# A hybrid attention layer on eight cores: the merge of the previous tile is written ahead of the GLA projections, and the order planner counts memory at 270 GB/s

## The chip, the cores and the metric

The kernel runs on the 8 cores of one Trainium2 chip. Each core works on one sequence of the batch of 8, and no core needs anything of another. The metric is the device time of the slowest core, in microseconds (us). Before the change it was 1416.05 us as the median of 3 runs (1414.8 to 1484.5).

## The reference

One decoder layer with two branches that share one input projection. For each token the columns of `w_in` give queries, keys, values and a gate for a causal differential attention with ALiBi (4 heads, two maps of 64), and queries, keys, values, a gate and a low-rank decay for gated linear attention (GLA, 4 heads, state 64 x 128). Both branch outputs are normed, gated, projected up, and merged under two sigmoid gates; an output projection, a norm and the residual follow.

```python
h = rms_norm(x, g_pre)
qa, ka, va, za, qb, kb, vb, zb, lr, gate_a, gate_b = split(h @ w_in)        # 1024 -> 5648
oa = diff_attention(qa, ka, va, lam, slopes)                                # causal, over all 4096 positions
ya = (rms_norm(oa, g_sub_a) * (1 - lam_init) * silu(za)) @ w_up_a           # 512 -> 1024
glog = log_sigmoid(lr @ w_alpha + b_alpha) / 16
ob = gla_chunked(qb, kb, vb, glog)                                          # a state carried from chunk to chunk
yb = (rms_norm(ob, g_sub_b) * silu(zb)) @ w_up_b                            # 512 -> 1024
y = sigmoid(gate_a) * ya + sigmoid(gate_b) * yb
out = x + rms_norm(y @ w_out, g_post)                                       # 1024 -> 1024
```

## The kernel before

**Tiles and stages.** The 4096 tokens of a core are worked in 8 tiles of 512, `t` = 0 to 7. A tile passes through these stages: `stage_a` (load x, norm, transpose to `hT`), `stage_batt` (the attention's Q, K and V projections, 96 matmuls of 512 columns), `stage_za` (the gate of the attention, 32), `stage_glaproj` (GLA's values, queries with keys, and gate: 32 each, and in a stream of its own the low-rank decay, 10), `stage_gla` (four chunks of 128 tokens that run through a state: in each, two matmuls for the scores, two for the new state, eight for the output), `stage_att` (attention of the tile over all keys so far: in batches of 8 score matmuls at L837, two exponentials on ACT at L845, then the matmuls into `acc`), `stage_e` (the merge: per column `j` of 8, two gate groups of 8 matmuls, then two up-projection groups of 4) and `stage_f` (output projection, 64 matmuls, norm, residual and store). `stage_e` and `stage_f` of tile t-1 run during tile t; those of tiles 0 and 1 both run during tile 2.

**Who sets the order.** The program does not issue instructions as it records them. `_Prog.op` records each with its duration on each engine that may take it, and `schedule` places them one by one: of all that are ready, the one that can start first; among those that start alike, the one with the lowest `prio`. A stream has a stretch of the plan, set by `P.at(begin, end, name)` in tiles, and `prio` runs linearly from begin to end by the PE work recorded in that stream so far. `fill(t)` is the stream from t to t+1 into which `stage_za`, `stage_glaproj`, `stage_e`, `stage_f` and the next tile's `stage_batt` are recorded one after the other, so the order of the calls in the main loop is the order of their due times; attention has the stretch t to t+1 as a stream of its own, the decay ("g") and GLA's chunks ("c") have theirs. What comes out is one fixed order for each engine and one for SP, which issues all DMAs.

**How a DMA is planned.** One transfer after the other, each `nbytes` at a fixed rate behind the one before, and 1.8 us until it has landed (L242). The rate decides only the order; it moves no data.

**Buffers that the steps touch.** Projections go through two PSUM banks (`pg`): a group fills one, ACT or DVE empties it. Scores use four banks (`qk`), written by a batch once both exponentials of the batch before have read them; `acc` has two. A weight chunk of 1 MB (bf16) lives in `wbuf`, three buffers from tile 2 on. The first time a chunk is needed it is converted (`convert`): eight f32 pieces of 256 KB through staging buffers in `KT`, each scaled by DVE, ACT or POOL, then stored to `wsc`, from where every later use loads it (`acquire`). GLA needs its keys transposed by DMA (`khat`, from `ktT`).

The softmax here doesn't subtract the row's maximum and nothing guards it: scores larger than these inputs give would overflow.

## Time and profile before

| | us |
|---|---|
| median of 3 runs | 1416.05 |
| fastest of them | 1414.8 |
| the profiled execution, whole | 1419.39 |
| span of its slowest core (core 1), first to last instruction | 1417.8 |
| spans of the other cores | 1399.1 to 1412.5 |
| PE busy on core 1 | 1329.9 |
| ACT busy | 830.6 |
| DVE busy | 742.2 |

The profile's page shows one execution on its slowest core. Engines are PE (matmul), PEld (weight load, beside PE), DVE, ACT, POOL and SP (DMA issue). Busy times are unions, and a matmul's end is modelled, so that the spacing of matmuls is read from start to start. Line L511 is a helper that records every matmul but the scores (L837); what a matmul is can be told from its tiles: `ps_pg<-sb_hT,sb_wbuf` is a projection by token rows (values, gates z, V), `ps_pg<-sb_wbuf,sb_hT` one by columns (Q, K, merge gates), `ps_pg<-sb_gaT,sb_wbuf` and `sb_gbT` the up-projections, `ps_pg<-sb_wbuf,sb_yT` the output projection, `ps_acc<-sb_V,sb_PT` attention's second matmul, `ps_pg<-sb_qtT,sb_ktT`, `sb_vb,sb_khat`, `sb_stbf,sb_qtT` and `sb_vb,sb_ATs` the four kinds of a GLA chunk. In the first tiles some buffers lie in the space of `KT`, `V` and `yT`, so `sb_V` can stand for `hT` or `gbT`, and `sb_yT` for a weight buffer.

### The profile page before, as it was taken

The numbers are of one execution on the slowest core, as the hardware profiler recorded it, in microseconds if no ns is written. First come the engines' busy times: TensorE is split into PE (matmuls) and PEld (weight loads), VectorE is DVE, ScalarE is ACT, GpSimd is POOL, SyncE is SP. The second block draws the span as 40 slices with busy tenths as digits, with TensorE's granted clock in tenths as the row PEclk, the third lists the DMA queues.
The fourth block names the chain that finished last, engine by engine and source line by source line (L and its number), as shares of the span: only waits on it lengthen the run. The fifth ranks groups of instructions, "written<-read, shape, count | busy, mean of one in ns | idle before, by whom it ended". The sixth has DMA issues, their size and how long they took to land.

```text
span 1417.8 us, 30361 instructions; the slowest of 8 cores (1399.1 to 1417.8 us)
## 1 busy us (share of the span) xinstructions
PE 1329.9 (94%) x10784; PEld 735.3 (52%) x10784; DVE 742.2 (52%) x2211; ACT 830.6 (59%) x1134; POOL 201.4 (14%) x309
## 2 busy tenths in 40 slices
PE   4997999999989999999989999999999999999996
PEld 2344454444545555545555555555555555666542
DVE  4488675666753557344472354643355624344634
ACT  4454556444535557475574766758666768767721
POOL 2142121010210012000120011210011200110100
PEclk9999999999999999999999999999999999999998
DMA  8995538955684328514294142743325722321443
GB/s 255 283 268 160 144 95 260 252 171 166 179 235 175 127 98 236 174 60 131 93 257 153 61 131 94 208 165 98 95 97 137 236 72 70 108 78 64 161 171 119
DMA packets 120099, 217.44 MB, mean 153 GB/s; under 512 B 73472, under 2 KB 82064, under 8 KB 105744
## 3 DMA queue, kind: packets, MB, share of 16 engines
q1 hardware_dynamic: 119952, 215.51, 50.3%
q8 instruction: 89, 1.46, 0.4%
q14 instruction: 58, 0.48, 0.1%
HBM read 166.72 MB, written 32.51 MB: 141 GB/s over the span
## 4 chain that ended last, share of the span: by engine, by line
PE 82%; DMA 6%; DVE 4%; issue 3%; ACT 3%; SPq 2%; POOL 0%; DVEq 0%; ACTq 0%; POOLq 0%
PE ps_pg L511 57%; PE ps_acc L511 15%; PE ps_qk L837 9%; DMA sb_KT<-w_in 2%; DMA sb_xr<-x 2%; ACT sb_PT L845 2%; DMA sb_khat<-sb_ktT 1%; SPq L488 1%; SPq L588 1%; DMA sb_wbuf<-wsc 1%; DVE sb_xr L974 0%; DMA sb_KT<-w_up_a 0%; DVE sb_szB L682 0%; DMA sb_KT<-w_out 0%; DMA wsc<-sb_wbuf 0%
## 5 line engine op out<-in xcount | busy, mean ns | idle before, releaser
L845 ACT ACTIVATE sb_PT<-ps_qk 128x1024 bf16<-128x1024 f32 (+1 forms) x544 | 518.0, 997 | 200.4 <-PE ps_qk L837 186.1
L511 PE MATMUL ps_acc<-sb_V,sb_PT 128*128 128x129 bf16 x4224 | 401.5, 221 | 8.2 <-ACT sb_PT L845 4.3
L511 PE MATMUL ps_pg<-sb_hT,sb_wbuf 128*128 128x512 bf16 x1536 | 392.3, 381 | 4.3 <-DVE sb_szB L682 1.3
L511 PEld LDWEIGHTS ps_acc<-sb_V,sb_PT 128*128 128x128 bf16 x4224 | 308.1, 98 | 139.5 <-issue 32.3
L511 PE MATMUL ps_pg<-sb_wbuf,sb_hT 128*128 128x512 bf16 x864 | 225.6, 380 | 4.5 <-DVE sb_szB L682 3.2
L511 PEld LDWEIGHTS ps_pg<-sb_hT,sb_wbuf 128*128 128x128 bf16 x1536 | 142.9, 98 | 150.9 <-issue 30.1
L837 PE MATMUL ps_qk<-sb_QT,sb_KT 64*128 64x256 bf16 (+1 forms) x2176 | 162.9, 269 | 10.9 <-ACT sb_PT L845 10.5
L945 DVE SCALAR_TENSOR_TENSOR sb_tmp<-sb_tmp,ps_pg 128x512 f32<-128x512 f32 x128 | 87.8, 686 | 142.5 <-PE ps_acc L511 85.7
L930 ACT ACTIVATE sb_tmp<-ps_pg 128x512 f32<-128x512 f32 x128 | 76.4, 597 | 131.3 <-PE ps_pg L511 98.2
L891 POOL TENSOR_TENSOR sb_statE<-sb_statE,sb_mhalf 128x1 f32<-128x1 f32 x128 | 75.0, 591 | 380.3 <-DVE sb_statE L889 369.7
L837 PEld LDWEIGHTS ps_qk<-sb_QT,sb_KT 64*128 64x128 bf16 x2176 | 84.5, 94 | 76.1 <-issue 57.5
L511 PEld LDWEIGHTS ps_pg<-sb_wbuf,sb_hT 128*128 128x128 bf16 x864 | 80.4, 98 | 80.8 <-issue 15.8
L511 PE MATMUL ps_pg<-sb_wbuf,sb_yT 128*128 128x512 bf16 x448 | 116.2, 385 | 5.3 <-DVE sb_tmp L965 2.2
L850 POOL TENSOR_SCALAR_AFFINE_SELECT sb_PT<-sb_PT 128x512 bf16<-128x512 bf16 x64 | 43.1, 673 | 501.9 <-ACT sb_PT L845 499.4
L511 PE MATMUL ps_pg<-sb_V,sb_wbuf 128*128 128x512 bf16 x288 | 70.9, 396 | 7.0 <-DVE sb_wbuf L595 1.5
L962 ACT ACTIVATE sb_tmp<-ps_pg 128x512 f32<-128x512 f32 x64 | 38.2, 597 | 50.4 <-PE ps_pg L511 33.9
L511 PEld LDWEIGHTS ps_pg<-sb_wbuf,sb_yT 128*128 128x128 bf16 x448 | 41.2, 99 | 48.3 <-issue 16.7
L511 PE MATMUL ps_pg<-sb_gbT,sb_wbuf 128*128 128x512 bf16 x224 | 61.8, 379 | 1.8 <-DVE sb_ste L792 0.7
L511 PE MATMUL ps_pg<-sb_gaT,sb_wbuf 128*128 128x512 bf16 x224 | 62.7, 380 | 0.1
L965 DVE TENSOR_TENSOR sb_tmp<-ps_pg,sb_gpost 128x512 f32<-128x512 f32 x64 | 43.9, 688 | 36.1 <-ACT sb_tmp L962 35.9
L681 ACT ACTIVATE sb_tmp<-ps_pg 128x512 f32<-128x512 f32 x64 | 37.9, 601 | 39.7 <-PE ps_acc L511 21.6
L893 DVE SCALAR_TENSOR_TENSOR sb_gatedA<-sb_oaf,sb_statE,sb_szA 128x128 bf16<-128x128 f32 x128 | 45.7, 360 | 21.6 <-POOL sb_statE L891 20.6
(135 smaller groups left out, 1260.6 us busy)
## 6 DMA issues: line engine op xcount, KB each, us to landing
sb_wbuf<-wsc SPq DMA_DIRECT2D x94, 1024.0 KB, 5.4
sb_KT<-w_in SPq DMA_DIRECT2D x88, 256.0 KB, 8.7
sb_xr<-x SPq DMA_DIRECT2D x36, 512.0 KB, 5.1
out<-sb_xr SPq DMA_DIRECT2D x32, 512.0 KB, 3.2
sb_xa<-x SPq DMA_DIRECT2D x28, 512.0 KB, 6.0
wsc<-sb_wbuf SPq DMA_DIRECT2D x14, 1024.0 KB, 7.0
sb_KT<-w_out SPq DMA_DIRECT2D x16, 256.0 KB, 4.5
sb_yT<-wsc SPq DMA_DIRECT2D x2, 1024.0 KB, 10.1
```

Of the source, the lines that this page charges most:

```text
L488: return P.op({"sp": (0.38, 0.0)}, lambda e: e.dma_start(out=fn_out(), in_=src), reads=reads, writes=writes, dma=sem, nbytes=nbytes)
L511: return P.op(_pe(n), lambda e: e.matmul(out=out_f(), lhsT=lf(), rhs=rf(), start=start, stop=stop, **kw), reads=reads, writes=writes, mode ...
L681: P.op({"act": _act(512, True)}, lambda e: e.activation(out=tmp[z.i][:], in_=pg[b.i][:], func=AF.Tanh, scale=0.5), table="tanh", reads=[b] ...
L837: lambda e, kb=kb, m=m, kbi=kbi, ca=ca, n=n: e.matmul(out=qk[:, 2 * half + m, kbi * 256:kbi * 256 + n], lhsT=KT[64 * m:64 * m + 64, h, kb ...
L845: P.op({"act": (0.075 + width / 600.0, 0.1)}, lambda e: e.activation(out=PT[pt.i][:, :, 0:width], in_=qk[:, 2 * half:2 * half + 2, 0:width ...
L850: return e.affine_select(out=v, in_=v, pattern=[[0, 2], [0, 2], [1, 128]], compare_op=ALU.is_ge, fill=0.0, base=0, channel_multiplier=-1)
L891: P.op({"pool": (0.45, 0.1)}, lambda e: e.tensor_tensor(out=statE[st.i][:, 4:5], in0=statE[st.i][:, 3:4], in1=mhalf[:, 0:1], op=ALU.pow), ...
L893: P.op({"dve": _dve(128, 1.0, 1)}, lambda e: e.scalar_tensor_tensor(out=gatedA[:, blk, h * 128:(h + 1) * 128], in0=oaf[o2.i][:], scalar=st ...
L930: P.op({"act": _act(512, True)}, lambda e, b=b, z=z: e.activation(out=tmp[z.i][:], in_=pg[b.i][:], func=AF.Tanh, scale=0.5), table="tanh", ...
L945: P.op({"dve": _dve(512)}, lambda e, b=b, z=tg[ab]: e.scalar_tensor_tensor(out=tmp[z.i][:], in0=tmp[z.i][:], scalar=1.0, in1=pg[b.i][:], o ...
L962: P.op({"act": (0.571, 0.02)}, lambda e, b=b, z=z, st=st, hh=hh: e.activation(out=tmp[z.i][:], in_=pg[b.i][:], func=AF.Square, accum_out=s ...
L965: P.op({"dve": _dve(512)}, lambda e, b=b, z=z, hh=hh: e.tensor_tensor(out=tmp[z.i][:], in0=pg[b.i][:], in1=gpost[:, hh * 512:(hh + 1) * 51 ...
```

## The change

In the main loop `stage_e` of the tiles `us` moves from behind GLA to the place between `stage_za(t)` and `stage_glaproj(t)`; `stage_f` stays behind GLA. The decay stream is due from t+0.3 to t+0.5 instead of t-0.05 to t+0.15, GLA's chunks from t+0.55 to t+1 instead of t+0.25 to t+0.95. The two chunks of `w_out` are no longer converted at the start of tile 2 but where `stage_f` first asks for them, so that tile 2 does not load them from `wsc` again. The planner's rate for transfers goes from 300 to 270 GB/s. Matmuls are the same 10784.

```diff
             if o.is_dma:
-                dma_free = max(dma_free, free[e]) + o.nbytes / 300e3
+                dma_free = max(dma_free, free[e]) + o.nbytes / 270e3
                 o.fin = dma_free + 1.8
...
-            P.at(t - 0.05, t + 0.15, "g")
+            P.at(t + 0.3, t + 0.5, "g")
...
         def stage_gla(t):
-            P.at(t + 0.25, t + 0.95, "c")
+            P.at(t + 0.55, t + 1, "c")
...
+            us = [u for u in (((), (), (0, 1))[t] if t < 3 else (t - 1,)) if u < ntiles]
             if t < ntiles:
                 stage_za(t)
-            if t == 2:
-                for c in (W_O, W_O + 1):
-                    convert(c, (0, 0.5))
+            if us:
+                stage_e(us, t)
             if t < ntiles:
                 stage_glaproj(t)
                 stage_gla(t)
                 fill(t)
-            us = [u for u in (((), (), (0, 1))[t] if t < 3 else (t - 1,)) if u < ntiles]
             if us:
-                stage_e(us, t)
                 stage_f(us)
```

What the two programs issue is shown at three places.

PE at the end of attention of tile 4 (scores in `ps_qk`, second matmuls in `ps_acc`, the Q projection of tile 5 as `ps_pg<-sb_hT,sb_wbuf`, or GLA's outputs from `sb_stbf` and `sb_ATs`); before:

```order
L837 MATMUL ps_qk<-sb_QT,sb_KT 128x256 x8
L511 MATMUL ps_acc<-sb_V,sb_PT 128x129 x6
L837 MATMUL ps_qk<-sb_QT,sb_KT 128x256 x8
L511 MATMUL ps_acc<-sb_V,sb_PT 128x129 x24
L511 MATMUL ps_pg<-sb_hT,sb_wbuf 128x512 x51
```

and with the change:

```order
L837 MATMUL ps_qk<-sb_QT,sb_KT 128x256 x8
L511 MATMUL ps_pg<-sb_hT,sb_wbuf 128x512 x8
L511 MATMUL ps_pg<-sb_stbf,sb_qtT 128x128
L511 MATMUL ps_acc<-sb_V,sb_PT 128x129 x5
L511 MATMUL ps_pg<-sb_vb,sb_ATs 128x128
L511 MATMUL ps_acc<-sb_V,sb_PT 128x129 x6
L511 MATMUL ps_pg<-sb_stbf,sb_qtT 128x128
L511 MATMUL ps_acc<-sb_V,sb_PT 128x129 x3
L837 MATMUL ps_qk<-sb_QT,sb_KT 128x256 x8
L511 MATMUL ps_pg<-sb_hT,sb_wbuf 128x512 x8
```

Before, two score batches have only six matmuls between them and the next tile's projections come behind the attention; with the change a projection group of eight stands between the same batches.

PE at the last two GLA chunks of tile 0 (the gate projection z of GLA is `ps_pg<-sb_wbuf,sb_V` here); before:

```order
L511 MATMUL ps_pg<-sb_vb,sb_khat 128x256 x2
L837 MATMUL ps_qk<-sb_QT,sb_KT 128x256 x6
L837 MATMUL ps_qk<-sb_QT,sb_KT 128x128 x2
L511 MATMUL ps_pg<-sb_stbf,sb_qtT 128x128
L511 MATMUL ps_pg<-sb_vb,sb_ATs 128x128
L511 MATMUL ps_pg<-sb_stbf,sb_qtT 128x128
L511 MATMUL ps_pg<-sb_vb,sb_ATs 128x128
L511 MATMUL ps_pg<-sb_stbf,sb_qtT 128x128
L511 MATMUL ps_pg<-sb_vb,sb_ATs 128x128
L511 MATMUL ps_pg<-sb_stbf,sb_qtT 128x128
L511 MATMUL ps_pg<-sb_vb,sb_ATs 128x128
L511 MATMUL ps_pg<-sb_wbuf,sb_V 128x512 x16
```

and with the change:

```order
L511 MATMUL ps_pg<-sb_wbuf,sb_V 128x512 x4
L511 MATMUL ps_pg<-sb_qtT,sb_ktT 128x256 x2
L511 MATMUL ps_pg<-sb_wbuf,sb_V 128x512 x4
L511 MATMUL ps_pg<-sb_vb,sb_khat 128x256 x2
L511 MATMUL ps_pg<-sb_wbuf,sb_V 128x512 x5
L511 MATMUL ps_pg<-sb_stbf,sb_qtT 128x128
L511 MATMUL ps_pg<-sb_vb,sb_ATs 128x128
L511 MATMUL ps_pg<-sb_stbf,sb_qtT 128x128
L511 MATMUL ps_pg<-sb_vb,sb_ATs 128x128
L511 MATMUL ps_pg<-sb_stbf,sb_qtT 128x128
L511 MATMUL ps_pg<-sb_wbuf,sb_V 128x512
L511 MATMUL ps_pg<-sb_vb,sb_ATs 128x128
```

The last sixteen matmuls of the gate projection, which stood behind the last chunk, stand between its steps.

SP at the start of tile 2, where weights are converted for the first time (`w_out` is the output projection, `w_in` in 2x256 the merge's gates, `w_up_a` and `w_up_b` the up-projections); before:

```order
L588 DMA sb_KT<-w_out 128x512 x8
L520 DMA_TRANSPOSE sb_gbT<-sb_gatedB 128x4x128
L588 DMA sb_KT<-w_out 128x512
L627 DMA wsc<-sb_wbuf 128x4096
L588 DMA sb_KT<-w_out 128x512 x2
L520 DMA_TRANSPOSE sb_gaT<-sb_gatedA 128x4x128
L588 DMA sb_KT<-w_out 128x512
L520 DMA_TRANSPOSE sb_gaT<-sb_gatedA 128x4x128
L588 DMA sb_KT<-w_out 128x512
L603 DMA sb_wbuf<-wsc 128x4096
L588 DMA sb_KT<-w_out 128x512 x3
L603 DMA sb_wbuf<-wsc 128x4096
```

and with the change:

```order
L588 DMA sb_KT<-w_in 128x2x256 x8
L520 DMA_TRANSPOSE sb_gbT<-sb_gatedB 128x4x128
L588 DMA sb_KT<-w_up_a 128x512 x4
L627 DMA wsc<-sb_wbuf 128x4096
L588 DMA sb_KT<-w_up_b 128x512
L520 DMA_TRANSPOSE sb_gbT<-sb_gatedB 128x4x128
L588 DMA sb_KT<-w_up_b 128x512 x3
L520 DMA_TRANSPOSE sb_gaT<-sb_gatedA 128x4x128 x2
L520 DMA_TRANSPOSE sb_gbT<-sb_gatedB 128x4x128
L627 DMA wsc<-sb_wbuf 128x4096
L588 DMA sb_KT<-w_in 128x2x256 x8
```

The merge's first two chunks take the place of the output projection's, and the two loads for GLA's projections that stood among them stand later.

## Rows read from the trace of the kernel before

**Rows 1.** The page, span and part 1: busy us, share, instructions
```profile
span 1417.8 us, 30361 instructions; the slowest of 8 cores (1399.1 to 1417.8 us)
PE 1329.9 (94%) x10784; PEld 735.3 (52%) x10784; DVE 742.2 (52%) x2211; ACT 830.6 (59%) x1134; POOL 201.4 (14%) x309
```
**Rows 2.** Windows: stretch, its us, busy us (count) by engine, PE clock, DMA, GB/s
```profile
0.00:40.00 40.00, 18.45 (x107) 9.67 (x108) 18.47 (x48) 19.51 (x31) 8.69 (x18) 0.99 0.92 260
40.00:120.00 80.00, 75.58 (x454) 36.09 (x453) 55.54 (x181) 38.66 (x57) 21.90 (x31) 0.96 1.06 270
120.00:200.00 80.00, 69.34 (x498) 36.71 (x500) 59.39 (x221) 39.29 (x56) 17.09 (x25) 0.93 0.39 114
200.00:400.00 200.00, 189.53 (x1290) 97.94 (x1290) 131.16 (x366) 99.81 (x150) 27.89 (x40) 0.99 0.69 200
400.00:760.00 360.00, 344.58 (x2715) 190.01 (x2714) 183.88 (x552) 208.64 (x293) 51.21 (x78) 1.00 0.52 159
760.00:1320.00 560.00, 549.57 (x5229) 326.19 (x5227) 248.60 (x747) 391.12 (x488) 67.44 (x104) 1.00 0.36 115
1320.00:1418.00 98.00, 82.85 (x503) 38.69 (x501) 45.13 (x100) 33.59 (x62) 7.17 (x13) 0.95 0.43 152
```
**Rows 3.** Waits of PE: who waited for whom, us, times, longest
```profile
PE ps_qk L837 <- ACT sb_PT L845: 10.5, 17, 1.5
PE ps_acc L511 <- ACT sb_PT L845: 4.3, 10, 1.0
PE ps_pg L511 <- DMA sb_khat<-sb_ktT: 2.9, 2, 2.1
PE ps_acc L511 <- DVE sb_oaf L883: 2.2, 4, 1.3
PE ps_pg L511 <- DMA sb_wbuf<-wsc: 0.3, 1, 0.3
```
**Rows 4.** Timeline of PE, end of tile 4's attention: start, us, what, idle before
```profile
735.64 0.59 PE L511 MATMUL ps_pg<-sb_wbuf,sb_yT 128*128 128x512 bf16 x2
736.07 0.27 PE L511 MATMUL ps_pg<-sb_vb,sb_khat 128*128 128x256 bf16 x1
...
738.41 0.62 PE L511 MATMUL ps_acc<-sb_V,sb_PT 128*128 128x129 bf16 x8
738.86 0.22 PE L511 MATMUL ps_pg<-sb_stbf,sb_qtT 128*128 128x128 bf16 x1
...
739.18 0.61 PE L837 MATMUL ps_qk<-sb_QT,sb_KT 64*128 64x256 bf16 x8
739.94 0.50 PE L511 MATMUL ps_acc<-sb_V,sb_PT 128*128 128x129 bf16 x6 [0.15 <-POOL sb_PT L850]
741.92 0.61 PE L837 MATMUL ps_qk<-sb_QT,sb_KT 64*128 64x256 bf16 x8 [1.47 <-ACT sb_PT L845]
```
**Rows 5.** Timeline of ACT, end of tile 3's attention
```profile
562.74 1.94 ACT L845 ACTIVATE sb_PT<-ps_qk 128x1024 bf16<-128x1024 f32 x2 [0.78 <-PE ps_qk L837]
```
**Rows 6.** Timeline of PE, GLA of tile 0
```profile
137.16 0.38 PE L511 MATMUL ps_pg<-sb_vb,sb_khat 128*128 128x256 bf16 x2 [1.49 <-DVE sb_cum L504]
...
139.77 0.26 PE L511 MATMUL ps_pg<-sb_stbf,sb_qtT 128*128 128x128 bf16 x1 [1.74 <-DVE sb_statB L806]
```
**Rows 7.** Windows in GLA of tile 0, columns as in group 2
```profile
128.20:131.60 3.40, 3.40 (x16) 1.84 (x16) 2.80 (x11) 0.94 (x2) 0.38 (x1) 0.50 0.09 17
131.60:138.40 6.80, 4.38 (x57) 2.97 (x54) 6.24 (x25) 4.04 (x7) 1.79 (x3) 1.00 0.00 1
138.40:145.20 6.80, 5.43 (x19) 2.46 (x20) 5.35 (x30) 1.56 (x3) 3.08 (x4) 0.50 0.10 22
```
**Rows 8.** Timeline of PE, tile 4: the longest wait for a transposed key
```profile
647.58 0.27 PE L511 MATMUL ps_pg<-sb_vb,sb_khat 128*128 128x256 bf16 x1 [2.05 <-DMA sb_khat<-sb_ktT]
```
**Rows 9.** DMA issues: out<-in, count, KB each, median us to landing
```profile
sb_KT<-w_in SPq DMA_DIRECT2D x88, 256.0 KB, 8.7
...
sb_gaT<-sb_gatedA SPq DMA_TRANSPOSE x24, 5.8
```
**Rows 10.** Windows of tile 2's conversions, columns as in group 2
```profile
205.80:241.00 35.20, 33.57 (x252) 17.97 (x251) 22.06 (x71) 23.46 (x32) 8.40 (x11) 1.00 0.84 251
241.00:340.00 99.00, 93.06 (x595) 46.47 (x594) 65.09 (x173) 42.08 (x59) 8.56 (x13) 0.99 0.75 218
```

## The prediction

> **What bounds the kernel now.** I read the page first. PE is busy 1329.9 of 1417.8 us [rows 1], no other engine over 830.6, so the span is PE's work plus what PE waits. The matmuls stay the same 10784; a change of order can only move the 88 us in which PE idles, and the clock. The windows show where those lie [rows 2]: 21.6 us in the first 40 (before the weights are there), 4.4 to 120, 10.7 to 200, 10.5 to 400, 15.4 to 760, 10.4 to 1320 and 15.2 in the tail. The head's order is hardly touched and the merge and output projection of tile 7 keep theirs, so 37 us are out of reach and some 51 are left, of which late tiles hold few: a gain of 2%, 28 us, would ask for over half of them.
>
> Then the waits of PE [rows 3]: score matmuls for the exponentials (10.5 us, 17 times), the second attention matmuls for the exponentials (4.3) and for the emptying of `acc` (2.2), GLA for transposed keys (2.9). Weight loads stand at 0.3: that a buffer comes free late costs nothing today, so looser loads alone win nothing.
>
> **How I price the new order.** Between a point that starts something and the point that needs it I count PE's instructions in each order. A 512-column matmul takes 0.215 us (two from 735.64 to 736.07), a 129-column one 0.056 (eight from 738.41 to 738.86) [rows 4]. Where that work is shorter than what has to happen meanwhile, the difference is a wait.
>
> **Scores behind exponentials, -5.8 us.** A score batch may start when two exponentials of the batch before are done; two take 1.94 us [rows 5], some 0.5 after the batch began, so less than 2.45 us of PE work between two batches is a wait. Before, tile 4 shows it: six matmuls of 0.056 between two batches, and 1.47 us idle [rows 4]. Of the 271 gaps 18 are short in the order before, by 11.3 us together; the trace has 10.5, so the count may be trusted. With the change 9 are short, by 5.1: the merge, due early, leaves projections for the end of the attention, where a group of eight (1.7 us) now stands. Scaled to the trace: 10.5 x 5.1 / 11.3 = 4.7, a gain of 5.8. With limits of 2.2 and 2.6 us the gain is 4.7 and 7.4.
>
> **The second attention matmuls, -2.8 us.** Batches whose exponentials have under 1.3 us before they are read go from 25 to 13 (7.7 to 4.2 us), changes of `acc` with under 1.5 us from 10 to 7 (4.7 to 2.9). Scaled to 4.3 and 2.2 [rows 3]: 2.0 and 0.8. Bounds: nothing, and all 6.5.
>
> **Keys, -2.0 us.** Nearly all of the 2.9 us is two waits, tile 4's 2.05 [rows 8] and one in tile 1. From the projection of the keys to the first use stand 7.1 and 7.2 us of PE work there, with the change 8.4 and 7.9: 1.3 + 0.7. In the other tiles the smallest is 7.4 in both orders, and 7.4 had no wait. Bounds: 0 and 2.9. This is what the slower rate in the planner can give. In the stretches where the queues are full the trace has 260 and 270 GB/s [rows 2], so 270 lands transfers where the chip does. The Trainium skill, "DMA: Bandwidth & Descriptors", Specifications, gives a limit of about 358 GB/s per core; by that 300 was already cautious, this term would be 0 and the sum 2 us higher. The trace does not come near 358.
>
> **GLA of tile 0, -2.0 us.** Its four chunks follow each other nearly uncovered: two waits, 1.49 and 1.74 us, on the DVE chain that empties one chunk's output [rows 6]. With the change sixteen matmuls of the gate projection stand inside, not behind; the work from first to last matmul of this GLA grows from 18.2 to 21.7 us. The most is 3.2, the least 0; I take 2.0, what the gaps gain against the chain.
>
> **What it adds, +3.1 us.** GLA is squeezed in every tile. In tile 2 it falls from 116 to 31.6 us of PE work, short by 1.2 of the 5.8 us that a chunk's output buffer needs; from tile 3 to 7 it keeps 46 to 73 us, enough. The two `pg` banks: groups that come before the bank is emptied add up to 20.1 us before and 22.0 with the change, +1.9. Bounds: 0, and twice that.
>
> **What costs nothing, and its cover.** The merge now reads attention's and GLA's outputs of the tile before soon after they are made: from the last of attention to its first use at least 17.8 us of PE work remain (57 to 69 in most tiles before), and 12.0 after the last GLA chunk of tile 7 (34.0 before). A transpose of such a tile lands in 5.8 us [rows 9] and a few DVE steps stand ahead; if that cover failed, gates and attention behind it on PE would all wait, some 2 us per tile. Loads of weights with under 9 us of PE work to come in fall from nine to four outside the tail. Two loads of `w_out` chunks in tile 2 go; they were hidden.
>
> **Sum.** -5.8 - 2.8 - 2.0 - 2.0 + 3.1 = -9.5 on the profiled execution's own 1419.4: 1409.9. The median of the runs shown is 1416.05, 3.3 under that execution, so I predict **1407 us**.
>
> **Rivals.** (1) *It does not do what it says*: waits leave one place and come back at the next, since DVE and ACT have the same work; my counts look at one pair of points at a time. For: the bank count rises. Against: the score count fits the trace. Time 1412 to 1421, as before.
>
> (2) *Conversions come late in tile 2*, the one that ends slower. At 205.8 SP starts with the merge's chunks. A chunk is eight pieces through four staging buffers; at 8.7 us to land [rows 9] and 0.7 to scale, two rounds take 18.8 us. Gate and up-projection chunk together take 37.6, and the second is needed 34 us of PE work after the first one's buffer is free (141.8 to 175.8). Half of it is enough to start, so I count no wait; but with landings of 11 us each of the five later chunks would be 4 to 5 us late, 22 together: 1429. For: DMA at 0.84 in that stretch [rows 10]. Against: two 1 MB loads that stood there are gone, and the six chunks need 20 MB, 92 us at the 218 GB/s of the stretch after, with 106 us of PE work (141.8 to 248.2). It decides below 188 GB/s.
>
> (3) *The clock, upwards.* In tile 0's GLA the granted clock is 0.50, the 1.2 GHz level, for 10.2 us [rows 7], after PE had idled 2.4 of 6.8 us, which costs 5.1 us. Squeezed GLA could bring that to later tiles: 5.1 us in tile 2 alone, up to 31 in six tiles; with two tiles 1417, and with all 1438. The Trainium skill, "TensorE: Matmul & The Clock Gate", HAM oscillation, says so: gaps between bursts let the clock fall to half, and the next burst starts cold. The trace agrees for tile 0. Against: only tile 2's GLA gets as bare as that.
>
> (4) *Faster than I think*: the half clock goes with the gaps of tile 0 (5.1), all of the 6.5 and 2.9 us go, and tile 2's 10.5 us [rows 2] halve: -9.5 - 5.1 - 4.6 - 5 = -24, 1392.
>
> **Chances.** Forecast (1400 to 1412) 0.46; no net change 0.22; (4) 0.13; (2) 0.12; (3) 0.07. A measurement of this kernel can tell about 2%, 28 us, from no change: under 1388 or over 1444. Faster holds about half of (4), 0.07; slower a third of (2) and a part of (3), 0.06; within 0.87. The range takes in the low end of the costs and most of (4), and above it (1) and half of (2): 1390 to 1428. The forecast's own range is 1400 to 1412.
>
> **What would show it.** Right: waits of score matmuls near 5 us and no long one at the ends of tiles 3 and 4; key waits under 1; a merge in tile 2 that starts near 230 us with PE over 0.95 busy to 400; windows from 760 on as before. Wrong: waits on `sb_wbuf` pieces between 225 and 330 us (2), clock rows of 0.50 outside tiles 0 and 7 (3), or a total idle within 4 us of 88 (1).

## The result, and the profile after

The changed kernel takes **1402.07 us** in the median of four runs (1400.61 to 1403.35), the kernel before 1415.42. The ratio is 0.9909, with a 95% interval of 0.9889 to 0.9928: a gain of 0.9%, under the 2% that the prediction counted as a change. The forecast was 1407, the range 1390 to 1428. The profiled execution took 1400.61 us. In some executions the cores of one die run at a lower granted clock and take longer (1484.5 us among the four of the kernel before): the medians here keep them, the ratios and the mean spans leave them out.

The page of the changed kernel, span and busy times, against [rows 1]:

```profile
span 1399.1 us, 30375 instructions; the slowest of 8 cores (1392.7 to 1399.1 us)
PE 1318.6 (94%) x10784; PEld 728.3 (52%) x10784; DVE 741.6 (53%) x2215; ACT 829.2 (59%) x1133; POOL 194.9 (14%) x306
```

PE idles 80.5 us instead of 87.9. It is also 11.3 us less busy with the same 10784 matmuls: a matmul that runs at a lower granted clock counts as busy for longer, and the slowest core before (core 1) ran at 0.987 of the clock, the one after (core 5) at 0.995. Over all eight cores the mean span falls from 1407.2 to 1395.7, by 11.5; the slowest falls by 18.7, since core 1 stood 10.7 above the mean before and core 5 stands 3.4 above it now. That core 1 was a bad case: over the 60 executions of the kernel before that the ratios use, the mean span of the cores is 1406.7 and the slowest core stands 7.2 above it, over the four of the changed kernel it is 1396.5 and 4.0. So 10.2 us of the gain are in the mean of the cores, and some 3 in that the cores lie closer together.

Its windows, columns as in [rows 2]:

```profile
0.00:40.00 40.00, 17.19 (x99) 9.00 (x100) 16.84 (x47) 16.86 (x28) 8.28 (x18) 1.00 0.92 263
40.00:120.00 80.00, 71.81 (x441) 34.92 (x442) 56.05 (x178) 36.24 (x53) 17.88 (x28) 0.98 1.00 265
120.00:200.00 80.00, 68.74 (x513) 36.38 (x511) 56.38 (x206) 41.83 (x59) 16.23 (x24) 0.98 0.44 127
200.00:400.00 200.00, 190.97 (x1334) 99.35 (x1332) 130.16 (x396) 103.54 (x152) 31.41 (x44) 1.00 0.63 183
400.00:760.00 360.00, 356.03 (x2824) 195.22 (x2822) 194.23 (x565) 212.28 (x301) 51.14 (x79) 1.00 0.54 167
760.00:1320.00 560.00, 549.88 (x5265) 326.29 (x5264) 249.10 (x743) 399.91 (x502) 64.07 (x103) 1.00 0.37 114
```

PE's idle time from 400 to 760 us falls from 15.4 to 4.0. From 40 to 120 it grows from 4.4 to 8.2. The waits of PE on this core, against [rows 3]:

```profile
PE ps_qk L837 <- ACT sb_PT L845: 9.3, 11, 2.5
PE ps_acc L511 <- ACT sb_PT L845: 4.3, 5, 1.3
PE ps_acc L511 <- DVE sb_oaf L883: 2.3, 4, 0.9
PE ps_pg L511 <- DMA sb_khat<-sb_ktT: 1.5, 1, 1.5
PE ps_pg L511 <- DVE sb_szB L682: 0.9, 3, 0.6
```

Scores wait less often (11 times, not 17) but once for 2.5 us; the waits of the second attention matmuls and of `acc` did not move, that for keys halved on this core. What fell by 5 us is the last row, the third largest of PE's waits before:

```profile
PE ps_pg L511 <- DVE sb_szB L682: 5.4, 8, 1.1
```

On the eight cores before, projections waited 5.0 to 7.0 us (mean 5.8) for a bank that DVE was emptying into `szB`, GLA's gate; now 0.3 to 0.9. The prediction does not list this wait; its term for the banks, +1.9, has the other sign.

**A measure by tile.** One core's waits vary too much to compare twelve programs, so I add up *lost time*: for every two matmuls that follow each other on PE, the distance of their starts less the distance that such a pair has where nothing waits (0.216 us for 512 columns, 0.056 for 129, some 0.095 more at a change to or from scores). It holds PE's waits and what a lower clock costs, and is given as the mean over the six cores whose records have all 10784 matmuls, by the tile whose attention is running. Time less lost time is 1314 to 1321 us in all the programs below, so it tells where the time went. One program profiled twice gave 82.0 and 82.7. But it comes from one execution, and the cores of one program differ: tile 2 loses 11.8 to 22.1 us on the six cores before, 9.6 to 12.8 with the change. So a difference of 2 us in one tile is not told from chance, and the last column gives a second measure, the mean span of the eight cores over all executions that the ratios use (4 to 10 of each program, 60 of the kernel before). The executions of one program lie within 3 to 8 us of each other, and the kernel before has 1405.3 to 1407.8 on the four chips of the experiments.

| us lost per core | before tile 0's first scores | tile 0 | 1 | 2 | 3 | 4 | 5 | 6 | 7 | tail | sum | time | mean span |
|---|---|---|---|---|---|---|---|---|---|---|---|---|---|
| before | 15.5 | 5.4 | 17.0 | 16.3 | 7.3 | 9.9 | 6.1 | 6.7 | 4.3 | 9.3 | 97.9 | 1415.4 | 1406.7 |
| changed | 19.0 | 7.2 | 17.5 | 10.4 | 3.9 | 4.0 | 6.1 | 3.1 | 7.0 | 8.9 | 87.0 | 1402.1 | 1396.5 |
| b_merge_first | 15.1 | 5.0 | 15.9 | 34.0 | 4.9 | 2.6 | 3.9 | 6.3 | 5.6 | 8.7 | 101.8 | 1420.0 | 1410.9 |
| b_merge_noconv | 16.0 | 5.1 | 16.7 | 14.5 | 8.2 | 2.9 | 4.0 | 6.8 | 5.1 | 9.0 | 88.4 | 1407.0 | 1397.2 |
| b_decay_gla_late | 16.3 | 5.3 | 16.3 | 26.0 | 10.4 | 7.1 | 5.4 | 4.8 | 4.1 | 8.9 | 104.7 | 1420.8 | 1409.9 |
| b_rate270 | 18.5 | 7.2 | 15.6 | 21.6 | 11.7 | 9.2 | 11.6 | 8.1 | 4.6 | 8.9 | 117.2 | 1436.4 | 1426.3 |
| b_no_ln | 15.8 | 5.1 | 15.3 | 16.2 | 7.2 | 8.3 | 4.7 | 5.4 | 4.2 | 9.7 | 92.0 | 1408.8 | 1401.0 |
| a_convert_early | 19.0 | 7.2 | 17.5 | 19.5 | 3.2 | 3.7 | 5.7 | 2.6 | 7.0 | 8.9 | 94.3 | 1408.9 | 1399.8 |
| a_old_stretches | 19.0 | 7.4 | 16.6 | 14.5 | 9.0 | 3.7 | 3.2 | 4.6 | 5.1 | 8.6 | 91.8 | 1406.8 | 1398.6 |
| a_rate250 | 17.5 | 15.6 | 22.5 | 13.8 | 9.9 | 2.5 | 5.3 | 2.7 | 7.2 | 9.9 | 106.8 | 1420.8 | 1414.2 |
| a_rate300 | 16.3 | 5.3 | 15.4 | 12.3 | 5.1 | 3.6 | 3.8 | 3.8 | 7.0 | 9.3 | 82.0 | 1398.3 | 1389.6 |
| a_rate330 | 17.2 | 9.2 | 10.1 | 17.9 | 6.4 | 3.0 | 3.7 | 4.0 | 7.6 | 9.6 | 88.7 | 1409.7 | 1399.4 |
| a_no_ln | 18.8 | 7.2 | 16.9 | 13.6 | 4.2 | 3.8 | 5.5 | 3.3 | 6.7 | 9.2 | 89.1 | 1403.6 | 1394.1 |

The change takes 10.9 us off the sum: 5.9 in tile 2 and 12.9 in tiles 3 to 6, and gives 5.3 back up to tile 0 and 2.7 in tile 7, which no experiment looked into.

### The profile page after: what moved, and what is told of

Same layout as the page of the kernel before. It is cut to its first block, busy times and chain, and to the rows that moved or that the text cites. A ratio compares the mean times of both kernels' runs of the same rounds, so it can differ in the third digit from the quotient of the medians.

```text
span 1399.1 us, 30375 instructions; the slowest of 8 cores (1392.7 to 1399.1 us)
## 1 busy us (share of the span) xinstructions
PE 1318.6 (94%) x10784; PEld 728.3 (52%) x10784; DVE 741.6 (53%) x2215; ACT 829.2 (59%) x1133; POOL 194.9 (14%) x306
## 4 chain that ended last, share of the span: by engine, by line
PE 87%; DVE 5%; issue 3%; DMA 3%; ACT 2%; SPq 0%; POOL 0%; DVEq 0%; ACTq 0%; POOLq 0%
PE ps_pg L511 61%; PE ps_acc L511 16%; PE ps_qk L837 10%; DMA sb_xa<-x 1%; ACT sb_PT L845 1%; DMA sb_khat<-sb_ktT 1%; DVE sb_gatedB L811 0%; DVE sb_tmp L945 0%; DVE sb_wbuf L595 0%; PE ps_pg L515 0%; DMA sb_KT<-w_in 0%; DMA sb_KT<-w_up_b 0%; DVE sb_gatedB L803 0%; DVE sb_xr L974 0%; DVE sb_oaf L883 0%
## 5 line engine op out<-in xcount | busy, mean ns | idle before, releaser
L511 PE MATMUL ps_acc<-sb_V,sb_PT 128*128 128x129 bf16 x4224 | 407.5, 220 | 7.2 <-ACT sb_PT L845 4.3
L511 PE MATMUL ps_pg<-sb_hT,sb_wbuf 128*128 128x512 bf16 x1568 | 406.4, 380 | 5.1 <-DVE sb_tmp L945 1.3
L511 PE MATMUL ps_pg<-sb_wbuf,sb_hT 128*128 128x512 bf16 x800 | 206.0, 379 | 2.7 <-DVE sb_vb L504 0.8
L945 DVE SCALAR_TENSOR_TENSOR sb_tmp<-sb_tmp,ps_pg 128x512 f32<-128x512 f32 x128 | 87.9, 687 | 220.9 <-PE ps_acc L511 144.9
L930 ACT ACTIVATE sb_tmp<-ps_pg 128x512 f32<-128x512 f32 x128 | 76.5, 597 | 117.2 <-PE ps_pg L511 82.3
L511 PE MATMUL ps_pg<-sb_wbuf,sb_yT 128*128 128x512 bf16 x448 | 110.0, 379 | 6.0 <-DVE sb_yT L947 1.8
L511 PEld LDWEIGHTS ps_pg<-sb_wbuf,sb_hT 128*128 128x128 bf16 x800 | 73.1, 98 | 70.6 <-issue 11.6
L511 PEld LDWEIGHTS ps_pg<-sb_wbuf,sb_yT 128*128 128x128 bf16 x448 | 41.0, 97 | 50.2 <-issue 12.8
L511 PE MATMUL ps_pg<-sb_gaT,sb_wbuf 128*128 128x512 bf16 x224 | 65.6, 379 | 0.4 <-issue 0.4
L878 DVE RECIPROCAL sb_statE<-ps_acc 128x2 f32<-128x2 f32 x128 | 19.5, 164 | 71.7 <-PE ps_acc L511 62.8
L681 ACT ACTIVATE sb_tmp<-ps_pg 128x512 f32<-128x512 f32 x64 | 38.0, 597 | 31.3 <-PE ps_pg L511 19.6
```

What stands on the lines that cost most here:

```text
L511: return P.op(_pe(n), lambda e: e.matmul(out=out_f(), lhsT=lf(), rhs=rf(), start=start, stop=stop, **kw), reads=reads, writes=writes, mode ...
L681: P.op({"act": _act(512, True)}, lambda e: e.activation(out=tmp[z.i][:], in_=pg[b.i][:], func=AF.Tanh, scale=0.5), table="tanh", reads=[b] ...
L878: P.op({"dve": _dve(2)}, lambda e: e.reciprocal(out=statE[st.i][:, 0:2], in_=acc[a][:, 0:260].rearrange("p (m c) -> p m c", m=2)[:, :, 128 ...
L930: P.op({"act": _act(512, True)}, lambda e, b=b, z=z: e.activation(out=tmp[z.i][:], in_=pg[b.i][:], func=AF.Tanh, scale=0.5), table="tanh", ...
L945: P.op({"dve": _dve(512)}, lambda e, b=b, z=tg[ab]: e.scalar_tensor_tensor(out=tmp[z.i][:], in0=tmp[z.i][:], scalar=1.0, in1=pg[b.i][:], o ...
```

## The experiments

Names that begin with b_ are the kernel before with something edited, those with a_ the changed kernel. Ratios are to the kernel before. One correction for reading the lines: the traces name `rhs` first and `lhsT` second, so `ps_pg<-sb_wbuf,sb_hT` is a projection by token rows (V, values and the gates z) and `ps_pg<-sb_hT,sb_wbuf` one by columns (queries, keys, merge gates), the other way round from the list under "Time and profile before".

**The logarithm's function tables.** In the trace of before, the gate's wait in tile 4 has its reason on ACT. PE's timeline of the kernel before (start, us, what, idle before):

```profile
622.99 0.59 PE L511 MATMUL ps_pg<-sb_wbuf,sb_hT 128*128 128x512 bf16 x2
624.60 0.38 PE L511 MATMUL ps_pg<-sb_wbuf,sb_hT 128*128 128x512 bf16 x1 [1.02 <-DVE sb_szB L682]
```

and ACT's ahead of it:

```profile
618.49 1.28 ACT L736 ACT_TABLE_LOAD   x1
619.78 1.06 ACT L736 ACTIVATE sb_gl<-sb_gl 128x1024 f32<-128x1024 f32 x1
620.74 1.00 ACT L845 ACTIVATE sb_PT<-ps_qk 128x1024 bf16<-128x1024 f32 x1
621.76 1.28 ACT L681 ACT_TABLE_LOAD   x1
623.06 0.60 ACT L681 ACTIVATE sb_tmp<-ps_pg 128x512 f32<-128x512 f32 x1
```

The decay's logarithm (L736) and the gate's Tanh (L681) want different function tables; each load takes 1.28 us, and the bank waits behind the second. (The Trainium skill, "ScalarE activation tables: per-element evaluation and per-set limits", What a function is on this engine, gives 1283 ns between functions of two sets; the trace agrees, 1.28 us. Exponentials ran behind either load without one of their own.) So the gate's bank is emptied at 624, and PE stands. The edit, in both kernels:

```diff
-e.activation(out=gl[:, :, :], in_=gl[:, :, :], func=AF.Ln, bias=1.0, scale=1.0), table="ln",
+e.activation(out=gl[:, :, :], in_=gl[:, :, :], func=AF.Identity, bias=0.0, scale=1.0), table="ln",
```

> The kernel before, its order unchanged, but the decay's logarithm on ACT (L736) is replaced by a copy (Identity), so that the decay itself is left out; what goes is the two function-table loads of 1.28 us in each tile (Ln for the decay, Tanh for the next gate), 16 loads in all before. Theory B, tables: in tiles 3 to 6 the two loads stand 3 to 4 us apart on ACT, right where GLA's gate projection waits for a bank; without them PE's waits for the gate (szB, 5.0 to 7.0 us a core before) fall under 1.5, the late exponentials behind them go too, 6 to 9 us in all: ratio 0.994 to 0.996. Theory A, order of the score batches alone: ACT has 590 us to spare, so the loads cost PE next to nothing: 0.999 to 1.001, waits for szB still over 4 us.

Measured: ratio 0.9935 (0.9903 to 0.9968), 1408.8 us; the trace has one table load, where there were 16. Lost time falls by 5.9, 4.4 of it in tiles 3 to 6, the mean span by 5.7, and waits for `szB` from 5.8 to 3.1 in the mean of the cores. So the loads do cost PE time although ACT is idle for 40% of the span, and about half of the gate's wait is theirs; the other half stays. That waits for `szB` would fall under 1.5 was wrong.

> The changed kernel, its order unchanged, with the decay's logarithm on ACT replaced by a copy (Identity): the decay itself is left out, and with it the two function-table loads per tile. In the kernel before the same edit took 5.9 us off PE's lost time. If the change gained by taking the two loads away from the gate's banks, little is left here: under 2 us, 1400 to 1402. If the loads have only moved and now hold up the exponentials (in the changed kernel PE waits 2.5 us in tile 1, 1.5 in tile 4 and 2.3 in tile 5 right behind such a load), 5 to 7 us go: 1395 to 1397.

Measured: ratio 0.9906 (0.9889 to 0.9923), 1403.6 us, lost time 89.1 against 87.0, mean span 1394.1 against 1396.5: 2 us more by one measure and 2 less by the other, so no gain that can be told, and not the 5 to 7 of the second case. What score matmuls lose falls by 1.2 and what the second attention matmuls lose by 3.8 per core, in the places that the second case named, but the merge loses 3.6 and GLA's projections 2.1 in their stead. The loads do hold up exponentials in the changed kernel, and taking them away brings next to nothing: by lost time a wait that goes comes back at the next, as the first rival of the prediction said.

**One part alone: the merge's place.**

```diff
             if t < ntiles:
                 stage_za(t)
             if t == 2:
                 for c in (W_O, W_O + 1):
                     convert(c, (0, 0.5))
+            if us:
+                stage_e(us, t)
...
             if us:
-                stage_e(us, t)
                 stage_f(us)
```

> The kernel before with one part of the change: the merge written ahead of GLA's projections; decay, GLA chunks, rate and the early conversion stay. Theory A, the merge's place carries the gain: 8 to 10 us of waits go, ratio 0.993 or less, as with the whole change. Theory B: the decay keeps its early place, and now a merge gate's Tanh stands one or two ACT instructions behind the logarithm in tiles 3 to 6, so the pair of table loads still meets a projection bank; only the score batches gain (short gaps 18/11.3 us to 10/7.4 by the count, -3.6 us) and the bank waits stay: ratio 0.997 to 0.998.

Measured: ratio 1.0036 (1.0009 to 1.0064), 1420.0 us, slower than before. By the time both theories fall; the tiles tell more. In tiles 3 to 6 lost time goes from 30.0 to 17.7, nearly what the whole change reaches (17.1), and waits for `szB` from 5.8 to 0.4 in the mean, although the two table loads stay together. So the merge's place does carry the gain there. In tile 2 it goes from 16.3 to 34.0. PE in that tile (core 4), first matmuls of attention with nothing between, then the merge's first gate group at 237.16:

```profile
226.68 0.61 PE L837 MATMUL ps_qk<-sb_QT,sb_KT 64*128 64x256 bf16 x8 [0.82 <-ACT sb_PT L845]
227.76 0.50 PE L511 MATMUL ps_acc<-sb_V,sb_PT 128*128 128x129 bf16 x6 [0.47 <-POOL sb_PT L850]
229.83 0.94 PE L837 MATMUL ps_qk<-sb_QT,sb_KT 64*128 64x256 bf16 x8 [1.56 <-ACT sb_PT L845]
...
237.16 3.61 PE L511 MATMUL ps_pg<-sb_V,sb_wbuf 128*128 128x512 bf16 x16 [0.45 <-DVE sb_wbuf L595]
```

The first gate group waits for the conversion of its weights (L595). Up to then attention runs alone and waits for its exponentials: of the 17.7 us that tile 2 loses more, attention's matmuls have 9.2. The output projection has 2.7; that less attention is left to stand between its groups is argued, not shown.

**The same without the early conversion of `w_out`.**

```diff
-            if t == 2:
-                for c in (W_O, W_O + 1):
-                    convert(c, (0, 0.5))
```

> The kernel before with the merge written ahead of GLA's projections and without the early conversion of w_out; rate 300 and the old stretches stay. With the early conversion kept, this move cost 17.7 us in tile 2 (PE's lost time there 34.0 us a core against 16.3 before) and gained 12.3 in tiles 3 to 6 (17.7 against 30.0). Theory D, conversions: the eight staged loads of each w_out chunk stand on SP ahead of the merge's first chunks, so that attention runs out of other work to stand between its batches; without them tile 2 loses 10 to 16 us, tiles 3 to 6 stay near 17.7, and the time is 1394 to 1400 (ratio 0.986 to 0.990). Rival E, the later decay and GLA stretches are what saves tile 2: it stays over 25 us and the time over 1410.

Measured: ratio 0.9952 (0.9936 to 0.9968), 1407.0 us. Tile 2 falls from 34.0 to 14.5; tiles 3 to 6 are at 21.9, worse than expected. The mean span falls by 13.7 against b_merge_first. Theory D holds for tile 2, the size in time was too high by 7 us at least. The same stretch of core 4 in windows (columns as in [rows 2]), with the early conversion in b_merge_first:

```profile
222.00:237.00 15.00, 9.09 (x104) 6.78 (x104) 11.47 (x40) 12.94 (x15) 3.83 (x6) 0.89 0.77 225
```

and without it in b_merge_noconv:

```profile
222.00:237.00 15.00, 14.32 (x88) 7.01 (x87) 9.17 (x25) 7.13 (x11) 1.96 (x3) 1.00 0.89 226
```

The DMAs move the same 225 GB/s in both; what differs is whose weights they bring. PE is busy 9.1 or 14.3 of 15 us. SP issues the first pieces of the merge's first chunk (core 4, b_merge_first, then b_merge_noconv) 20 us apart:

```profile
221.48 2.15 SPq L588 DMA_DIRECT2D sb_KT<-w_in  x3
...
200.89 6.82 SPq L588 DMA_DIRECT2D sb_KT<-w_in  x8
```

The kernel before without the early conversion, and the merge where it was, was not run; whether the 19.5 us need the merge in front stays open. The counterpart is the changed kernel with the three lines put back behind `stage_za`:

> The changed kernel with the early conversion of the two w_out chunks put back at the start of tile 2, all else as changed. Theory D: tile 2 goes from 10.4 us lost on PE to between 24 and 34, and the time from 1402 to 1416 to 1426: the whole gain is gone. Rival E, the later stretches save tile 2: it stays under 16 us and the time under 1408.

Measured: ratio 0.9956 (0.9939 to 0.9973), 1408.9 us. Tile 2 goes from 10.4 to 19.5, in the direction of theory D and under its range; half of the gain in time is gone (6.8 us), and a third of the gain in the mean span (3.3 of 10.2), not all. Of the 9.1 us, merge groups lose 3.5 and the output projection 5.3; attention's matmuls lose 1.8 more and GLA 1.5 less. Rival E falls too, since 19.5 is over 16.

**The stretches of decay and GLA.** Alone on the kernel before:

```diff
-            P.at(t - 0.05, t + 0.15, "g")
+            P.at(t + 0.3, t + 0.5, "g")
...
-            P.at(t + 0.25, t + 0.95, "c")
+            P.at(t + 0.55, t + 1, "c")
```

> The kernel before with the two later stretches alone (decay t+0.3 to t+0.5, GLA chunks t+0.55 to t+1); merge, rate and conversion as before. Theory B: the logarithm now stands ahead of a merge gate (one to three ACT instructions in tiles 3 to 6), the two table loads stay together, waits for the gate of GLA become waits of the merge groups; score gaps 18/11.3 to 13/6.8 by the count, -4 us: ratio 0.997. Theory C, the decay's place alone carries the gain: 0.993 or less, no pair of table loads within 5 us in tiles 3 to 6.

Measured: ratio 1.0025 (0.9999 to 1.0051), 1420.8 us: theory C falls, and theory B's 0.997 with it, since neither looked at tile 2. The time may be that of the kernel before, the mean span is 3.2 longer. Tile 2 goes from 16.3 to 26.0, most of it waits of the merge (6.1 to 10.0) and of the output projection (4.8 to 9.8); tiles 3 to 6 gain 2.3 only. Taken back in the changed kernel (the same lines reversed):

> The changed kernel with the old stretches of decay and GLA chunks, at 270 GB/s. If the later stretches bring something of their own in tiles 3 to 6 (function tables 15 us apart, theory B), these tiles go from 17.1 us lost to 22 or more, 1407. If the place of the merge has already taken the gate's groups out of the way (theory A, as the merge alone gave 17.7 in these tiles), they stay within 16 to 20; by the count the score batches get worse in tile 1 (short gaps 9/5.1 to 11/7.8 us), so 1402 to 1406.

Measured: ratio 0.9947 (0.9926 to 0.9968), 1406.8 us. Lost time 91.8 against 87.0, tiles 3 to 6 at 20.5, of which 9.0 in tile 3: between the two expectations. So the later stretches cost when alone and bring 4.8 us a core once the merge is in front and the early conversion gone (6.4 at 300 GB/s: 88.4 in b_merge_noconv, 82.0 in a_rate300; by the mean span 2.1 and 7.6). Decay and GLA's chunks were not moved one without the other. Why tile 3 takes most of it was not tried.

**The planner's rate.** One number each: 270 in the kernel before, 300, 330 and 250 in the changed one.

```diff
-                dma_free = max(dma_free, free[e]) + o.nbytes / 270e3
+                dma_free = max(dma_free, free[e]) + o.nbytes / 300e3
```

> The kernel before with the planner's rate at 270 GB/s alone. As the prediction has it, the keys gain 2 us and nothing else changes: 1413. By the counts over the order it is worse: short score gaps 18/11.3 to 28/18.7 us, exponentials read too early 25/7.7 to 41/17.3, and the first 120 us lose the 3 to 5 us that the changed kernel lost there: 8 to 20 us slower, 1423 to 1435.

Measured: ratio 1.0154 (1.0126 to 1.0181), 1436.4 us, over 20 us slower than the kernel before. The counts over the order had the direction and, but for 1 us, the size (1423 to 1435); the prediction's reading of the rate was wrong. Every stretch up to tile 6 but tile 1 and 4 gets worse.

> The changed kernel with the planner's rate back at 300 GB/s, all else as changed. If the rate is what gave the keys their cover and nothing else, as the prediction has it, this costs 2 us: waits for transposed keys up by 1.5 to 2 us and the time 1404. If the rate of 270 is what makes the first 120 us worse (PE's excess there is 26 to 29 us with the change, 20 to 23 before), the head comes back to 20 to 23, the short score gaps are 6/3.1 us by the count instead of 9/5.1, and the time is 1396 to 1399, under the changed kernel by 3 to 6 us.

Measured: ratio 0.9871 (0.9819 to 0.9923), 1398.3 us; lost time 82.0. The first case falls: the time goes down, not up. The second holds, 2.7 us to tile 0, 1.9 in tile 0, 2.1 in tile 1; tile 2 loses 1.9. Where the head's part comes from, in PE's timeline; the changed kernel (core 1) first:

```profile
35.02 0.59 PE L511 MATMUL ps_pg<-sb_lrT,sb_walpha 128*128 128x512 bf16 x2 [0.95 <-ACT sb_lrT L503]
36.63 0.61 PE L515 MATMUL ps_pg<-sb_ident,sb_hb 128*128 128x128 bf16 x8 [1.02 <-ACT sb_gl L734]
38.20 0.61 PE L515 MATMUL ps_pg<-sb_ident,sb_hb 128*128 128x128 bf16 x8 [0.97 <-ACT sb_gl L736]
40.09 1.01 PE L511 MATMUL ps_pg<-sb_hT,sb_wbuf 128*128 128x512 bf16 x2 [1.28 <-DVE sb_hT L504]
40.89 3.62 PE L511 MATMUL ps_pg<-sb_V,sb_wbuf 128*128 128x512 bf16 x8
```

and at 300 GB/s (core 1):

```profile
34.33 0.38 PE L511 MATMUL ps_pg<-sb_lrT,sb_walpha 128*128 128x512 bf16 x1 [0.39 <-ACT sb_lrT L503]
34.89 0.38 PE L511 MATMUL ps_pg<-sb_lrT,sb_walpha 128*128 128x512 bf16 x1 [0.18 <-DVE sb_hT L504]
37.44 0.70 PE L515 MATMUL ps_pg<-sb_ident,sb_hb 128*128 128x128 bf16 x8 [2.17 <-DVE sb_hb L666]
38.65 8.32 PE L511 MATMUL ps_pg<-sb_V,sb_wbuf 128*128 128x512 bf16 x32 [0.52 <-DVE sb_wbuf L595]
```

At 270 both matmuls of the decay take both banks ahead of two groups of transposes, and the first of these waits for ACT to empty its bank. (The second is put down to L736, which reads no bank; what it transposes, `sb_hb`, was written up to 37.95.) In all four waits, 4.2 us, against 3.3. The eight matmuls at 40.89 take 3.4 us to the next start, twice their usual 1.7, as a window of the changed kernel (core 1) shows:

```profile
39.20:46.00 6.80, 5.91 (x14) 2.05 (x15) 3.38 (x5) 1.39 (x2) 0.00 (x0) 0.50 0.99 267
```

The granted clock is 0.50, the 1.2 GHz level, for 6.8 us. Summed over such stretches (length times what the clock lacks of 1, an upper bound, since PE idles in part of them), the first 120 us cost 3.7 us a core with the change and 2.0 at 300 GB/s.

> The changed kernel with the planner's rate at 330 GB/s. Theory F, the counts over the order tell the time: the five sums of the prediction (score gaps, exponentials read early, accumulators, projection banks, GLA chunks) are 47.5 us before, 37.1 with the change, 32.9 with the change at 300, and 25.5 here; over the nine programs measured so far PE's lost time follows them with a slope of 1.13, so 75 us lost against 82.0 at 300 and 87.0 at 270: 1389 to 1394. Theory G, the planner must know the chip's own rate (260 to 270 GB/s where the queues are full): a faster rate orders loads too late, waits for weights appear (over 5 us) and the time is 1400 or more.

Measured: ratio 0.9957 (0.9943 to 0.9972), 1409.7 us, lost time 88.7, where the counts gave 75. Theory F falls here: tile 1 gains 5.3, but tile 0 and tile 2 lose 3.9 and 5.6 against 300. Theory G has the time but not the reason for which it gave it: weights loaded from `wsc` cost 0 to 2.2 us on the eight cores (mean 0.5), not over 5; conversions (L595) cost 1.6 to 3.5 (mean 2.5).

> The changed kernel with the planner's rate at 250 GB/s, below what the chip moves in the stretches where the queues are full. Theory F: the five sums come to 57.4 us, lost time 108 to 112 us, time 1420 to 1428, slower than the kernel before. Theory G: a rate a little under the chip's own is as good as its own: 1400 to 1406.

Measured: ratio 1.0029 (1.0016 to 1.0042), 1420.8 us, lost time 106.8. Theory F has the time (1420 to 1428) and is 1.2 too high in lost time (108 to 112), theory G falls. Here 38 us are lost in tiles 0 and 1, where the change at 270 loses 25.

So of four rates 300 is the best, and 270 costs 4 us of time against it. To see whether that is more than chance:

> The changed kernel with the planner's rate at 300 GB/s once more, in more rounds. In its first comparison it stood at 0.9871 of the kernel before with an interval of 0.9819 to 0.9923, too wide to tell it from the changed kernel (0.9909, 0.9889 to 0.9928). If the 5.0 us that its PE lost less per core (82.0 against 87.0) are real time, the ratio is 0.986 to 0.989 and PE's lost time again 80 to 84; if they were chance of one chip, it comes out at 0.990 to 0.992, with 85 to 89 us lost.

Measured: ratio 0.9886 (0.9864 to 0.9907), 1398.2 us, lost time 82.7. It is the first case. A version with all of the change but the rate is thus the best one run, by 4 us in the medians and 4.3 to 5.0 us in lost time over the changed kernel; the intervals of the ratios still overlap. The mean spans do not: 1387.3 to 1392.6 in its ten executions, 1395.4 to 1398.5 in the four of the changed kernel.

## Why the prediction held, and where it did not

The time, 1402 against 1407, lay in the range, and the share of the sum (10.9 us lost less per core, 9.5 forecast) too. But the sum came out by terms that failed on both sides, so that it came so near was in part luck; and the 3 us by which the cores lie closer together have no term at all. Step by step, in lost time per core where a tile or a kind of matmul can be told:

**Scores behind exponentials (-5.8).** Measured -3.8 (12.6 to 8.8). Where the prediction looked it was right: in tiles 3 and 4 the waits fall from 6.6 to 0.2. The place of [rows 4] in the changed kernel:

```profile
727.73 0.61 PE L837 MATMUL ps_qk<-sb_QT,sb_KT 64*128 64x256 bf16 x8
728.27 1.90 PE L511 MATMUL ps_pg<-sb_hT,sb_wbuf 128*128 128x512 bf16 x8
...
731.06 0.61 PE L837 MATMUL ps_qk<-sb_QT,sb_KT 64*128 64x256 bf16 x8
731.61 1.90 PE L511 MATMUL ps_pg<-sb_hT,sb_wbuf 128*128 128x512 bf16 x8
```

No wait is left between these batches. But in tiles 1, 5 and 6 scores lose 2.9 more than before. The step that failed is that an exponential starts when its scores are there. It also stands in ACT's queue, behind whatever was ordered ahead of it. ACT in tile 1, then in tile 5 of the changed kernel:

```profile
161.41 1.28 ACT L736 ACT_TABLE_LOAD   x1
162.70 1.06 ACT L736 ACTIVATE sb_gl<-sb_gl 128x1024 f32<-128x1024 f32 x1
163.78 1.28 ACT L681 ACT_TABLE_LOAD   x1
165.07 1.08 ACT L681 ACTIVATE sb_tmp<-ps_pg 128x512 f32<-128x512 f32 x2
166.04 1.03 ACT L845 ACTIVATE sb_PT<-ps_qk 128x1024 bf16<-128x1024 f32 x1
...
840.67 1.06 ACT L659 ACTIVATE sb_hb<-sb_xa 128x1024 bf16<-128x1024 f32 x1 [1.16 <-DMA sb_xa<-x]
841.64 0.19 ACT L659 ACTIVATION_READ_ACCUMULATOR sb_hb<-sb_xa 128x1 f32 x1
841.73 1.00 ACT L845 ACTIVATE sb_PT<-ps_qk 128x1024 bf16<-128x1024 f32 x1
```

and the score matmuls of PE that wait for them:

```profile
167.22 0.56 PE L837 MATMUL ps_qk<-sb_QT,sb_KT 64*128 64x256 bf16 x8 [2.52 <-ACT sb_PT L845]
...
842.88 0.61 PE L837 MATMUL ps_qk<-sb_QT,sb_KT 64*128 64x256 bf16 x8 [1.67 <-ACT sb_PT L845]
```

In tile 1 two table loads stand ahead of it, in tile 5 a square of the next tile's x (L659), whose load had not landed: ACT idles 1.16 us with an exponential behind it that could run. (Without the loads, in a_no_ln, tile 1's scores lose 1.3 us less, tile 5's the same.) That the merge's place, with the early conversion gone, carries this term is shown by b_merge_noconv, where scores lose 6.6 and the second matmuls 7.0 less than before; the later stretches and the rate of 270 put part of the first and all of the second back.

**The second attention matmuls (-2.8).** Measured +0.4 (10.7 to 11.1). The same step failed: of the table loads' places, the one at 685 us in tile 4 alone costs such a matmul 1.3 us, and without the loads (a_no_ln) these matmuls lose 3.8 less.

**Keys (-2.0).** Waits for `khat` are 1.2 us in the mean of the eight cores before and 1.3 after. The 2.9 of [rows 3] were those of core 1 alone; other cores had 0.2 to 2.4. Taking one core's longest wait for a property of the order was the error. And the sentence that 270 "lands transfers where the chip does" earned nothing: by b_rate270 and a_rate300 the rate costs time in either kernel. Its sign was wrong: 4 to 5 us lost against the -2.0. The page of the Trainium skill by which this term would have been 0 came nearer ("DMA: Bandwidth & Descriptors", Specifications, some 358 GB/s). The 260 to 270 of [rows 2] are means over 40 and 80 us. In shorter stretches the chip moved more, in the kernel before too, so that "the trace does not come near 358" holds for those means alone. Seven us of the kernel before (core 1; 304 to 326 on its eight cores) and of the changed one (core 3):

```profile
35.00:42.00 7.00, 4.02 (x24) 1.80 (x23) 5.29 (x9) 4.30 (x7) 0.74 (x1) 0.82 1.02 304
35.00:42.00 7.00, 3.23 (x27) 1.70 (x24) 5.30 (x12) 4.25 (x8) 1.21 (x2) 0.78 1.03 332
```

That the planner does best at 300 was found by trial; 330 was worse again.

**GLA of tile 0 (-2.0).** GLA's matmuls lose 6.6 us before and 7.0 after in the stretch where they run (tile 1's attention). With the same stretches at 300 GB/s it is 2.4, and 2.7 with the later stretches alone, so they can bring the gain, but not in the order that 270 gives.

**What it adds (+3.1).** Tile 2's GLA loses 1.2 us more (1.0 to 2.2), the number that was forecast, but not by the squeeze: with the later stretches alone it loses 0.6, with the merge alone in front 2.4. The banks were forecast at +1.9; without the head, projections (17.5 to 11.2), merge (13.5 to 9.6) and output projection (11.2 to 8.6) lose 12.8 less. This is the largest error of the sum, and what paid for the terms that failed. The count gave every bank a fixed time to be emptied; the wait behind 622.99 above shows that the time depends on what else stands in ACT's queue. With the merge alone in front the waits for `szB` are down to 0.4 us; that GLA's gates then no longer meet the busiest stretch is argued, not shown.

**What costs nothing.** That two loads of `w_out` chunks go was put at nothing, "they were hidden". By a_convert_early the early conversion is worth 9.1 us of lost time in tile 2, 6.8 us of time and 3.3 of the mean span, by b_merge_noconv 19.5, 13.0 and 13.7. They were hidden from the waits for weights, but they set when the merge's own weights come, and so what work stands beside attention.

**What was out of reach.** "The head's order is hardly touched" was wrong: it loses 3.5 us up to the first scores and 1.8 in tile 0, and gets 2.7 and 1.9 of that back at 300 GB/s.

**The rivals.** (2), late conversions in tile 2, did not come in the changed kernel, yet it is what makes b_merge_first slower than before, from the order of conversions at 225 GB/s, above the 188 from which the prediction would have it. (3), the clock: the rows of 0.50 in tile 0's GLA [rows 7] are gone on all six cores. Three of them have one of 3.4 us at 168 us instead, behind the long score wait of tile 1, one has one at 369, and all have 3.4 to 6.8 us between 38 and 46, two one at 94. So it moved, mostly ahead; by the prediction's own sign (rows of 0.50 outside tiles 0 and 7) it shows in tile 1 and once in tile 2, at 1.7 us each, and not in the squeezed GLA of later tiles. Of the 10.2 us in [rows 7], 3.4 stand ahead of the idle stretch that the prediction names as their cause. (1), no net change, holds for single waits, as a_no_ln shows, and not for the sum.

**What was to be seen.** Right: no long score wait at the ends of tiles 3 and 4; PE over 0.95 busy from 240 to 400 (153.8 of 160 us); the window from 760 to 1320 as before (549.9 busy against 549.6); the merge in tile 2 starts near 230 (at 228.5); no wait for converted pieces between 225 and 330 on any core. Wrong: score waits of 5 (9.3 on the slowest core, 5.3 to 9.3 on the eight, mean 7.0), key waits under 1 (1.5).

## What to carry to other kernels

Count the work between a start and its use over the whole order, and add a second count: what stands ahead of the freeing instruction in its own engine's queue, table loads and instructions that wait for a transfer among them. A part of a change is not worth the same alone: here the merge in front and the later stretches each brought nothing by themselves (1.0036 and 1.0025), and the merge began to pay with the third part, the conversion that had been put at nothing. The rate with which a planner counts transfers is a knob to be tried on the chip, not a figure of the chip to be entered: the trace moved 260 to 270 GB/s on the mean and 304 to 332 over 7 us, and of 250, 270, 300 and 330 it was 300 that gave the best order.

## What the runs showed of the hardware that had not been expected

Two function-table loads of 1.28 us per tile on an engine that is busy 59% of the time cost the kernel before 5.9 us of PE time per core; in the changed order taking the same loads away changed lost time and mean span by 2 us, with opposite signs. The granted clock makes the cores of one execution unequal. Counted as above (an upper bound), the slowest core of the kernel before has 19.7 us, of which 5.4 in five stretches at 0.81, and stood 10.7 us above the mean of the cores; the others with full records have 8 to 14, and in the changed kernel all lie between 7 and 10.4.
